# Another order of the token tiles, and the last tile's k ahead of its q, in a two-layer attention kernel

## What is computed

```python
q = (rmsnorm(q_lat, qc_g) @ w_q_up).reshape(b, n, MLA_HEADS, QK_DIM)
kv = (rmsnorm(kv_lat, kvc_g) @ w_kv_up).reshape(b, n, MLA_HEADS, NOPE_DIM + V_DIM)
q_nope = rmsnorm(q[..., :NOPE_DIM], qn_g)
q_rope = rmsnorm(q[..., NOPE_DIM:], qr_g)
k_nope = rmsnorm(kv[..., :NOPE_DIM], kn_g)
v = kv[..., NOPE_DIM:]
...
s = jnp.einsum('bqhd,bkhd->bhqk', q_nope, k_nope) + jnp.einsum('bqhr,bkr->bhqk', q_rope, k_rope)
p = jax.nn.softmax(s.astype(jnp.float32), axis=-1).astype(v.dtype)
```

## Time and profile before

| | us |
|---|---|
| median of 3 runs | 1454.85 |
| the runs | 1454.08, 1454.85, 1457.75 |
| the profiled execution | 1455.48 |
| its span | 1453.6 |
| TensorE busy | 1415.8 (97%) |
| VectorE, ScalarE, GpSimd busy | 996.5 (69%), 519.7 (36%), 86.6 (6%) |
| projection stage of layer 0 | 139.6 to 179.3 |
| projection stage of layer 1 | 947.9 to 982.6 |

### The profile page before, as it was taken

One profiled execution on the slowest core, in us unless ns is written; L12 is line 12 of the kernel. 1 busy time (PEld: TensorE's weight loads), 2 busy tenths in 40 slices (PEclk: granted clock), 3 DMA queues, 4 the chain that ended last, 5 costly groups with the idle time before them and its releaser, 6 DMA issues.

```text
span 1453.6 us, 20613 instructions
## 1 busy us (share of the span) xinstructions
PE 1415.8 (97%) x7936; PEld 1223.5 (84%) x7936; DVE 996.5 (69%) x1523; ACT 519.7 (36%) x831; POOL 86.6 (6%) x125
## 2 busy tenths in 40 slices
PE   6999899999999999999999999989999999999998
PEld 3788798889888888888888878868998888888887
DVE  5587887779866666666575688788667555555555
ACT  4252865243231122212221325476445323223331
POOL 0023700000000000000000000350000000000000
PEclk9999999999999999999999999999999999999999
DMA  9742012323543233324333411301032222222323
GB/s 386 290 137 88 1 44 73 142 91 118 185 145 119 93 120 119 124 82 152 115 101 101 144 44 61 114 15 57 2 103 90 100 94 97 97 87 91 111 97 134
DMA packets 42983, 158.62 MB, mean 109 GB/s; under 512 B 5168, under 2 KB 6576, under 8 KB 41776
## 3 DMA queue, kind: packets, MB, share of 16 engines
q1 hardware_dynamic: 42928, 157.87, 31.4%
HBM read 155.76 MB, written 2.10 MB: 109 GB/s over the span
## 4 chain that ended last, share of the span: by engine, by line
PE 85%; DVE 8%; ACT 3%; DMA 2%; issue 1%; SPq 0%; ACTq 0%; DVEq 0%
PE ps L713 68%; PE ps L649 4%; PE ps L650 4%; PE ps L651 4%; DMA ada_step<-in_w_step 1%; DVE w_lo L1378 1%; DVE tmp L1487 1%; PE ps L663 1%; PE ps L863 1%; DVE nmax L1700 1%; DVE H_lo L1496 1%; DVE pt_lo L1502 1%; ACT prob L1237 1%; DVE part_sums L1649 1%; ACT w_hi L1050 0%
## 5 line engine op out<-in xcount | busy, mean ns | idle before, releaser
L713 PE MATMUL ps<-H_hi,w_hi 128*128 128x512 f32 (+1 forms) x1280 | 449.0, 351 | 3.8 <-DVE H_lo L1496 1.5
L713 PE MATMUL ps<-H_lo,w_hi 128*128 128x512 f32 (+1 forms) x1280 | 447.4, 350 | 0.0
L713 PE MATMUL ps<-H_hi,w_lo 128*128 128x512 f32 (+1 forms) x1280 | 447.1, 349 | 0.0
L1050 ACT ACTIVATE w_hi<-w_raw 128x1024 fp32r<-128x1024 f32 x180 | 187.5, 1055 | 422.1 <-PE ps L713 368.5
L713 PEld LDWEIGHTS ps<-H_hi,w_hi 128*128 128x128 f32 x1280 | 242.3, 189 | 37.8 <-DVE H_lo L1496 3.1
L713 PEld LDWEIGHTS ps<-H_hi,w_lo 128*128 128x128 f32 x1280 | 242.2, 189 | 31.5
L713 PEld LDWEIGHTS ps<-H_lo,w_hi 128*128 128x128 f32 x1280 | 242.3, 189 | 30.9
L1509 DVE SCALAR_TENSOR_TENSOR X<-ps,mod,X 128x512 f32<-128x512 f32 (+1 forms) x296 | 180.9, 645 | 109.2 <-PE ps L713 87.3
L1378 DVE TENSOR_TENSOR w_lo<-w_raw,w_hi 128x1024 fp32r<-128x1024 f32 x180 | 221.3, 1239 | 35.1 <-ACT w_hi L1050 34.1
L713 PE MATMUL ps<-inner_hi,w_hi 128*128 128x512 f32 (+1 forms) x528 | 187.6, 355 | 0.3 <-DVE X L1509 0.3
L713 PE MATMUL ps<-inner_lo,w_hi 128*128 128x512 f32 (+1 forms) x528 | 187.2, 355 | 0.0
(11 more groups left out here) (202 smaller groups left out, 1836.5 us busy)
## 6 DMA issues: line engine op xcount, KB each, us to landing
w_raw<-in_w_main SPq DMA_DIRECT2D x182, 512.0 KB, 3.2
ada_raw<-in_w_ada SPq DMA_DIRECT2D x73, 512.0 KB, 4.2
ada_step<-in_w_step SPq DMA_DIRECT2D x7, 2048.0 KB, 14.7
X<-in_x SPq DMA_DIRECT2D x2, 1024.0 KB, 6.9
cb<-in_cvec SPq DMA_DIRECT2D x2, 1024.0 KB, 7.2
...
```

What stands on the lines that cost most here:

```text
L713: ins = pe.matmul(job.ps(a, b), ww[:, wsl], xx[:, xk, a:b], start=first and n == 0, stop=last and n == 2)
L1050: act.activation(w_hi[c % 4][:], w_raw[c % 2][:], ACT.Copy).then_inc(chunk_hi, 1)
```

## The change

The tiles are projected in another order: 0, 1, 4, 5, 2, 3 in layer 0, and 4, 5, 0, 1, 2, 3 in layer 1. The code now counts positions n in this order (`TOKEN_ORDER` gives the tile). A tile has a q by `has_q`: all in layer 0, positions 2 to 5 in layer 1. At the last position (`LAST`, 5) the kv projection comes ahead of the q projection, and the k part ahead of the q part on ScalarE and VectorE. `turn(LAST)` turns k alone; the plain q of the last tile is turned by a job of its own, `turn_q`, behind s(0,1), and its rope part behind that. The rope turn of position 4 moves behind s(0,0). Each score takes the ctx keys ahead of the x keys. The waits for the last q's parts move to s(1,0) and s(1,1). There is one PSUM job more per layer; the matmuls are the same in number and size.

```diff
+TOKEN_ORDER = ((0, 1, 4, 5, 2, 3), (4, 5, 0, 1, 2, 3))
+LAST = TOK - 1
+def has_q(L, n):
+    return L == 0 or n >= TOK - XTOK
...
 def job_plan():
...
         for t in range(TOK + 1):
-            for kind in ("q", "kv"):
-                if t < (nq if kind == "q" else TOK):
+            for kind in ("kv", "q") if t == LAST else ("q", "kv"):
+                if t < TOK and (kind == "kv" or has_q(L, t)):
                     add((kind, t), L)
...
-            if t > 1 and t - 2 < nq:
+            if 1 < t < TOK and has_q(L, t - 2):
                 add(("rope", t - 2), L)
...
-        for name in (("s", 0, 1), "pool0", "pool1"):
+        for name in (("s", 0, 0), ("rope", LAST - 1), ("s", 0, 1), "turn_q", ("rope", LAST), "pool0", "pool1"):
...
             def score(u, i):
...
-                parts = [(t, 0, NX, 0), (t, NX, NT, NX)]
+                work = [(t, NX, NT, NX), (t, 0, NX, 0)]
                 if with_ctx(L, u):
-                    parts.append((XTOK + i, NX, NT, NT))
+                    work.insert(1, (XTOK + i, NX, NT, NT))
+                if u == 1 and i == 0:
+                    Job(JOB[("rope", LAST - 1), L]).taken(pe)
+                if u == 1 and i == 1:
+                    Job(JOB["turn_q", L]).taken(pe)
+                    Job(JOB[("rope", LAST), L]).taken(pe)
...
-            for t in range(2, TOK):
-                if t < qtok(L):
-                    project_q(t)
-                project_kv(t)
...
+            for n in range(2, TOK):
+                if n == LAST:
+                    project_kv(n)
+                    project_q(n)
+                else:
+                    if has_q(L, n):
+                        project_q(n)
+                    project_kv(n)
+                turn(n - 1)
+                if has_q(L, n - 2):
+                    turn_rope(n - 2)
+            turn(LAST)
...
             score(0, 0)
-            if TOK - 1 < qtok(L):
-                turn_rope(TOK - 1)
+            turn_rope(LAST - 1)
             score(0, 1)
+            turn_last_q()
+            turn_rope(LAST)
             pool_project(0)
             pool_project(1)
...
+            def stats(n):
+
+                if n == LAST:
+                    stats_k(n)
+                    value_hi(n)
+                    root_part(n, "k")
+                    stats_q(n)
+                    return
...
+            for kind in ("rope", "nope"):
+                root_part(LAST, kind)
+            turned_hi(LAST, "k")
             act.activation(warm[:, 0:1], ones[:, 0:1], ACT.Exp)
...
             exponentials(0, 0)
             exponentials(0, 1)
+            turned_hi(LAST, "q")
+            rope_out(LAST)
...
+            sums_k(LAST)
+            normed_k(LAST)
+            turned_lo(LAST - 1, part_order(L, LAST - 1, ("q",)))
+            value_lo(LAST)
+            sums_q(LAST)
+            turned_lo(LAST, ("k",))
+            normed_q(LAST)
             for i in range(2):
                 maxima(0, i)
+            turned_lo(LAST, ("q",))
             for i in range(2):
                 probabilities(0, i)
```

More of the change, by code:

```diff
@@ L70, with q_before @@
 NV = V_EPS + 1
+TOKEN_ORDER = ((0, 1, 4, 5, 2, 3), (4, 5, 0, 1, 2, 3))
+LAST = TOK - 1
+def has_q(L, n):
+    return L == 0 or n >= TOK - XTOK
+def q_before(L, n):
+    return sum(has_q(L, m) for m in range(n))
 def job_plan():
@@ L343, in V, with part_order, parts, sections @@
         return vec[:, L * V_LAYER + off:L * V_LAYER + off + n]
[L347 to L360 removed]
+    def part_order(L, n, q_kinds):
+        kinds = q_kinds if has_q(L, n) else ()
+        return ("k",) + kinds if n == LAST else kinds + ("k",)
+    def parts(L, n, kind):
+        return n + q_before(L, n) + 1 + part_order(L, n, ("q",)).index(kind)
+    def sections(L, n, kind):
+        return n + 2 * q_before(L, n) + 1 + part_order(L, n, ("rope", "nope")).index(kind)
+    def columns_of(L, n):
+        return slice(P * TOKEN_ORDER[L][n], P * (TOKEN_ORDER[L][n] + 1))
     def with_ctx(L, u):
@@ L614, in _ @@
             rotate(latr[:, :, QR + KVR:LATW], TOK, 2, kr_rot[L], 0, scratch)
-            for t in range(qtok(L)):
+            for n in range(TOK - qtok(L), TOK):
+                t = q_before(L, n)
                 pool.wait_ge(q_nm[L], t + 1)
@@ L623, in _ @@
                 if t > 1:
-                    Job(JOB[("rope", t - 2), L]).ready(pool)
+                    Job(JOB[("rope", n - 2), L]).ready(pool)
                 src = qn[t % 2][:, 0:ROPES].rearrange("p (h f) -> p h f", h=HEADS)
-                cos, sin = (rtab[:, n, t].unsqueeze(1).to_broadcast([P, HEADS, ROPE]) for n in range(2))
+                cos, sin = (rtab[:, e, TOKEN_ORDER[L][n]].unsqueeze(1).to_broadcast([P, HEADS, ROPE]) for e in range(2))
                 def halves(x):
@@ L637, in _ @@
                 pool.wait_ge(b_rot[L], 5 * t + 3)
[L638 removed]
+                hi, lo = (q_rs[L][t % 2][:, :, ROPE * e:ROPE * (e + 1)] for e in range(2))
                 pool.tensor_copy(hi.bitcast(F32R), src).then_inc(b_rot[L], 1)
@@ L837, in score @@
                 job.open(pe)
-                parts = [(t, 0, NX, 0), (t, NX, NT, NX)]
+                work = [(t, NX, NT, NX), (t, 0, NX, 0)]
                 if with_ctx(L, u):
-                    parts.append((XTOK + i, NX, NT, NT))
-                for qt, ka, kb, o in parts:
-                    if u == 0 and i == 0 and qt < XTOK:
-                        Job(JOB[("turn", (XTOK if ka == 0 else TOK) - 1), L]).taken(pe)
-                        Job(JOB[("rope", XTOK - 1), L]).taken(pe)
-                    if u == 0 and qt >= XTOK:
-                        Job(JOB[("rope", qt), L]).taken(pe)
+                    work.insert(1, (XTOK + i, NX, NT, NT))
[4 more added lines that the diff above has]
+                    Job(JOB[("rope", LAST), L]).taken(pe)
+                for qt, ka, kb, o in work:
+                    if (u, i) == (0, 0):
+                        Job(JOB[("turn", LAST if ka == 0 else LAST - 1), L]).taken(pe)
                     qs = slice(P * qt, P * (qt + 1))
@@ new lines, in turned_hi, with rope_out @@
+            def turned_hi(n, kind):
+                job = Job(JOB["turn_q" if (n, kind) == (LAST, "q") else ("turn", n), L])
+                job.ready(act)
+                dst, o, scale = (q, 0, qg[:, 0:1]) if kind == "q" else (k, 512, V(L, V_KN))
+                act.activation(dst[0][:, :, columns_of(L, n)], job.ps(o, o + 512).rearrange("p (h f) -> p h f", h=HEADS), ACT.Copy,
+                               scale=scale).then_inc(b_hi[L], 1)
+            def rope_out(n):
+                if has_q(L, n):
+                    job = Job(JOB[("rope", n), L])
+                    job.ready(act)
+                    job.last_read(act.activation(qrs[:, :, columns_of(L, n)], job.ps(0, 512).rearrange("p (h f) -> p h f", h=HEADS),
@@ new lines, in sums_k, with normed_q @@
+            def sums_k(n):
+                dve.wait_ge(b_sq[L], parts(L, n, "k"))
+                sums(n, "k", kn[n % 2][:], NOPE)
+            def normed_q(n):
+                inverse(n, "rope", "nope")
+                Job(JOB[("q", n), L]).taken(dve)
+                x = qn[n % 2][:, 0:ROPES].rearrange("p (h f) -> p h f", h=HEADS)
+                r = part_rms[:, n % 2, 0:4].unsqueeze(2).to_broadcast([P, HEADS, ROPE])
+                dve.tensor_tensor(x, x, r, ALU.mult).then_inc(q_nm[L], 1)
@@ new lines, in turned_lo @@
+            def turned_lo(n, kinds):
+                tsl = columns_of(L, n)
+                for kind in kinds:
+                    job = Job(JOB["turn_q" if (n, kind) == (LAST, "q") else ("turn", n), L])
+                    dst, o, scale = (q, 0, qg[:, 0:1]) if kind == "q" else (k, 512, V(L, V_KN))
+                    dve.wait_ge(b_hi[L], parts(L, n, kind))
+                    ins = lo_half(dst[1][:, :, tsl], job.ps(o, o + 512).rearrange("p (h f) -> p h f", h=HEADS),
+                                  dst[0][:, :, tsl], scale)
```

208 lines of the change are left out of this document (90 added, 118 removed).

## The result

The changed kernel takes **1463.70 us** (median of 6 runs, 1462.57 to 1466.84), the kernel before 1455.07 us beside it: ratio 1.0063, 95% interval [1.0053, 1.0073]. It is slower by 8.6 us. The forecast was 1461.2 us, range 1457 to 1466, slower with a chance of 0.68. The profiled execution took 1463.21 us, its span is 1461.3 us against 1453.6.

A forecast was written before the change was run, and what follows sets the result against it. TensorE, busy in 97% of the span, was taken as the bound, with almost no slack in the attention loops. Delays of s(1,0), +2.7 us in layer 0 and +3.8 in layer 1, added 6.5 to 1454.85: 1461.2 us, range 1457 to 1466.

The forecast's parts named there:

- layer 0, up to the end of s(0,0): Layer 0's projection tail: v_lo holds q5 and the slot for k5's turn, so s(0,0) ends 0.65 us later.
- layer 0, from there to s(1,0): Layer 0 behind s(0,0): late q waits for GpSimd, then slots wait for exponentials and q_lo; +2.05 us.
- layer 1, up to the end of s(0,0): Layer 1's projection stage: ctx tiles first, then q5's long chain; s(0,0) ends at 981.9 instead of 980.89, +1.0 us.
- layer 1, from there to s(1,0): Layer 1 behind s(0,0): added turn of q5 and a 1.5 us GpSimd wait before the rope turn; +2.8 us.
- Layer 1, the start: Layer 1's first projections: TensorE waits 3.0 us for GpSimd's rotation, while VectorE begins about 1.1 us earlier.
- The clock: Three waits of about 3 us might drop TensorE's clock, 1.4 us per fall on the path; none in the sum.
- rival 3: Long waits in both layers: the clock falls in one to three of them, 1462.6 to 1465.4 us; chance 0.15.
- rival 4: Whole kernel: the forecast itself, 1459.2 to 1463.5 us without a clock fall; chance 0.53.
- Rivals 1 and 2: Whole kernel: faster, at most 5.1 us won, chance 0.07; or waits move, within 0.3%, 1457 to 1458 us, chance 0.25.
- Rival 1: Both layers' tails: early k5 removes waits of 1.87 and 0.68 us, at most 5.1 us, 1449.8; chance 0.07.

The follow-up runs named there:

- e12: Changed kernel with the wait before the last k's turn filled as in e2, and layer 1's first q projection ahead of k_rope's turn: 1460.51 us, ratio 1.0036.
- e5: Changed kernel with the last q served earlier on VectorE and ScalarE, position 4's rope turn ahead of s(0,0), last q's turn ahead of s(0,1): 1458.39 us.
- e2: Changed kernel with 11 unread 128x512 matmuls per layer added in the wait before the last tile's k is turned: 1460.54 us, ratio 1.0036.
- e9: Kernel before, with the first piece of layer 1's latent projection multiplied three times instead of once: 1455.04 us, ratio 0.9996.
- e10: Changed kernel, but last q projected first, k still turned first, layer 1's first q projection forward, nine unread matmuls per layer filling tail waits: 1453.34 us.
- e11: The changes of e9 and e10 together in one kernel: 1454.06 us, ratio 0.9991.
- e6: e5 with layer 1's first q projection moved ahead of the turn of k_rope: 1457.23 us, ratio 1.0016.

## Why the prediction was right, and where it was not

Sign and range were right, and so was the mechanism of each step in the sum. The total is not the sum's doing alone: the sum came out 0.7 us too high, and falls of the clock that it did not hold added 2.8. e12 is the kernel that the sum described, since the sum had no fall in it; its terms can be held against it.

| term | forecast | e12 | changed kernel |
|---|---|---|---|
| layer 0, up to the end of s(0,0) | +0.65 | +0.62 | +0.86 |
| layer 0, from there to s(1,0) | +2.05 | +2.01 | +2.00 |
| layer 1, up to the end of s(0,0) | +1.0 | +0.37 | +1.49 |
| layer 1, from there to s(1,0) | +2.8 | +2.80 | +4.31 |
| sum | +6.5 | +5.8 | +8.7 |

(Each is the start of the rope turn or score behind s(0,0), less the stage's start, less the same of before: 36.91 and 32.88.)

*Layer 0.* q5 was to wait for v_lo and start at 166.70: 165.60 + 1.11 = 166.71. k was to be turned at 173.35: 173.32. The wait for GpSimd before the last rope turn was to be 0.75: 0.57, and 0.73 in e12. These are queues of instructions with known durations, and laying them out one by one held to a tenth or two.

*Layer 1, the start.* The wait of 3.0 us came (2.76) and was hidden, as the text said, by VectorE's earlier start. The term that was mis-sized is what was left of it, "+1.0 us" up to the end of s(0,0), laid out with VectorE at 4.3 to 4.7 us a tile; undisturbed it is 0.4. By that layout q5 was to start at 971.4 (done at 973.85, less 2.36 and 0.1); it started at 972.42 - 1.54 = 970.88, in the times of before's trace, and in e12, counted the same way, at 970.77.

*Layer 1, to s(1,0).* A wait of 1.5 us for GpSimd: in e12 1.30. In the changed kernel it is absent, because TensorE at half clock came late enough to find q_rs done.

*The clock.* This is the part that failed. The text put the falls outside the sum, at 1.4 us each and a chance of 0.15. What happened is rival 3, and 1463.70 lies within its 1462.6 to 1465.4, just above the 1459.2 to 1463.5 that rival 4, the forecast without a fall, allowed. Without falls in its stages, as e12, it takes 1460.51. Two things in that reasoning were off. The row that spoke against a fall, the sparse tail of layer 1 with 2.07 of 4.6 us busy at 1.00, consists of several waits of 0.5 to 1.4 us, none as long as the 2.91 us that the change was itself predicted to make; the nearer row, a wait of 2.51 us at 872 with the clock at 0.50 behind it, was in the trace of before, and the argument left it out. And one price for all falls is wrong: it was 0.2 us in layer 0 of the changed kernel (another wait stood behind it), 1.56 in layer 0 of e5, 2.6 in the tail of layer 1 (41.75 against 39.12), 1.7 at the start of layer 1 (e2 against e12), 0 to 0.7 at 872 (e9), and for the fall at 23.10 itself, priced at 1.4, 1.1 (139.65 against 138.54). Of the Trainium skill's rule (TensorE: Matmul & The Clock Gate, section "Why this matters for your kernels"), that long idle gaps between bursts bring the half clock, the traces bear out the direction: each fall in the two stages stands behind a gap of 1.6 us or more, and filling the gaps of the tails kept the clock up there in e2 and e10 to e12. They don't bear out that a gap always does it: the 2.76 us wait brought a fall in five of seven traces.

*Rivals 1 and 2* fell with the late q. Rival 1's gain shows where q comes early and the clock stays: up to the end of s(0,0) in layer 0 it is 0.84 us in e10, 0.85 in e11 and 0.54 in e6.
